# Two weight units interleaved k-tile by k-tile at the start of both feed-forward stages

## The reference

```python
h = rmsnorm(x, norm_ffn_g[layer]) * (1 + scale2) + shift2
x = x + gate2 * conv_ffn(h, w_ffn_gate[layer], w_ffn_up[layer], ffn_conv[layer], w_ffn_down[layer])

def conv_ffn(h, w_gate, w_up, conv, w_down):
    u = dwconv3(h @ w_gate, conv)
    return (jax.nn.silu(u) * (h @ w_up)) @ w_down
```

## Time and profile before

| | |
|---|---|
| median of 3 runs | 1585.81 us (1580.39 to 1587.88) |
| the profiled execution's own time | 1583.95 us |
| its span, first to last instruction | 1581.9 us |
| mean granted TensorE clock | 0.959 of full |
| TensorE busy | 1430.3 us (90%) |
| VectorE busy | 995.3 us (63%) |
| GpSimd busy | 658.7 us (42%) |

### The profile page before, as it was taken

The page is one execution under the profiler, slowest core; times in us unless marked ns, Lnnn a source line. Parts: engine busy times, 40 slices in busy tenths (PEclk is TensorE's granted clock), DMA queues, the critical chain, the costliest instruction groups (busy, mean ns, idle before and its releaser), DMA issues.

```text
span 1581.9 us, 24703 instructions
## 1 busy us (share of the span) xinstructions
PE 1430.3 (90%) x9517; PEld 1384.4 (88%) x9517; DVE 995.3 (63%) x1377; ACT 418.9 (26%) x725; POOL 658.7 (42%) x400
## 2 busy tenths in 40 slices
PE   3798789989868789999999999986999999999995
PEld 2598768989858689999999999975999999999995
DVE  5695477983568777687777888635655145415554
ACT  4615322146341253300110011156332011101122
POOL 0262344430204335555545555410454544455542
PEclk9799889999979889999999999998999999999998
DMA  9221411240213313543334433210332122222222
GB/s 377 94 94 53 147 40 41 90 151 28 79 73 142 120 54 126 189 146 138 123 116 149 146 138 121 83 45 1 102 110 93 67 80 79 65 82 70 75 70 78
DMA packets 44358, 161.13 MB, mean 102 GB/s; under 512 B 4752, under 2 KB 5904, under 8 KB 43280
## 3 DMA queue, kind: packets, MB, share of 16 engines
q1 hardware_dynamic: 44304, 160.43, 28.8%
HBM read 153.07 MB, written 5.77 MB: 100 GB/s over the span
## 4 chain that ended last, share of the span: by engine, by line
PE 75%; DVE 13%; issue 4%; ACT 4%; DMA 2%; POOL 1%; ACTq 0%; SPq 0%; DVEq 0%; POOLq 0%
PE ps L653 64%; PE ps L938 1%; DVE ada_raw L1430 1%; PE ps L665 1%; DVE outer L1620 1%; ACT work L1007 1%; DVE junk L1430 1%; DVE work L1447 1%; DVE blocks L1623 1%; PE ps L880 1%; PE ps L685 1%; DVE work L1350 1%; ACT work L1136 1%; PE ps L890 1%; DVE x L1385 1%
## 5 line engine op out<-in xcount | busy, mean ns | idle before, releaser
L582 POOL TENSOR_SCALAR whi<-raw 128x1024 fp32r<-128x1024 f32 (+1 forms) x172 | 192.3, 1118 | 763.9 <-PE ps L653 565.8
L653 PE MATMUL ps<-hhi,whi 128*128 128x320 f32 x1984 | 460.4, 314 | 52.4 <-DVE hlo L1414 31.0
L653 PE MATMUL ps<-hlo,whi 128*128 128x320 f32 x1984 | 455.7, 311 | 0.0
L653 PE MATMUL ps<-hhi,wlo 128*128 128x320 f32 x1984 | 455.2, 311 | 0.0
L585 POOL TENSOR_TENSOR wlo<-raw,whi 128x1024 fp32r<-128x1024 f32 (+1 forms) x172 | 435.6, 2532 | 14.4
L653 PEld LDWEIGHTS ps<-hhi,whi 128*128 128x128 f32 x1984 | 334.5, 190 | 61.4 <-issue 26.4
L653 PEld LDWEIGHTS ps<-hlo,whi 128*128 128x128 f32 x1984 | 335.5, 190 | 0.0
L653 PEld LDWEIGHTS ps<-hhi,wlo 128*128 128x128 f32 x1984 | 335.4, 190 | 0.0
L653 PE MATMUL ps<-hidhi,whi 128*128 128x320 f32 x704 | 161.2, 310 | 4.5 <-POOL wlo L585 3.1
L653 PE MATMUL ps<-hidlo,whi 128*128 128x320 f32 x704 | 161.0, 310 | 0.0
L653 PE MATMUL ps<-hidhi,wlo 128*128 128x320 f32 x704 | 160.9, 310 | 0.0
(11 more groups left out here) (205 smaller groups left out, 1318.7 us busy)
## 6 DMA issues: line engine op xcount, KB each, us to landing
raw<-in_w_gu SPq DMA_DIRECT2D x88, 512.0 KB, 3.2
ada_raw<-in_w_rows SPq DMA_DIRECT2D x75, 512.0 KB, 3.4
raw<-in_w_in SPq DMA_DIRECT2D x28, 512.0 KB, 3.3
raw<-in_w_dn SPq DMA_DIRECT2D x32, 448.0 KB, 3.3
ada_first<-in_w_ada SPq DMA_DIRECT2D x4, 2048.0 KB, 21.1
raw<-in_w_dn SPq DMA_DIRECT2D x16, 512.0 KB, 3.3
raw<-in_w_out SPq DMA_DIRECT2D x8, 512.0 KB, 4.6
x<-in_x SPq DMA_DIRECT2D x1, 2560.0 KB, 9.0
```

Source lines behind the costliest of these rows:

```text
L582: nc.gpsimd.tensor_scalar(whi[s][:, 0:n], raw[s][:, 0:n], 1.0, 0.0, ALU.mult, ALU.add).then_inc(s_whi, 1)
L653: last = nc.tensor.matmul(pair[pr][:, b], wt[s][:, cs], act[:, k, b * HALF:(b + 1) * HALF], start=(j == 0 and q == 0), stop=(j == len(tile ...
```

## The change

Three things, the same in both layers.

1. `first_units` takes units 0 and 1 together. For each k-tile TensorE waits for the normed tile k, makes unit 0's product of k (pair A), then unit 1's product of k-1 (pair B). After the last tile it makes unit 1's last product. Then come units 2 and 3, one after the other, outside the loop; the loop goes on from pair 2.
2. Unit 2 is split into a third pair of buffers (`whi2`, `wlo2`), laid over the last part of `rows_tok`, which the second layer's mixer uses.
3. The split of unit 2 has no guard on unit 0 any more; in its place POOL waits for the last normed tile (`s_h`). The split of unit 3 keeps its buffer and its guard: units 0 and 1 must both have been multiplied.

```diff
+        whi.append(nc.alloc_sbuf_tensor_at("whi2", [P, SLOT], F32R, offset=o4 - 8 * SLOT))
+        wlo.append(nc.alloc_sbuf_tensor_at("wlo2", [P, SLOT], F32R, offset=o4 - 4 * SLOT))
...
-            def split(u, half_u, s, n=SLOT, guard=True):
+            def split(u, half_u, s, n=SLOT, guard=True, to=None):
+                to = s if to is None else to
                 pool.wait_ge(s_raw[s], half_u * 16 + 16)
                 if guard:
                     pool.wait_ge(s_unit, u - 1)
...
+            def second_pair(u):
+                split(u + 2, u // 2 + 1, 0, guard=False, to=2)
+                split(u + 3, u // 2 + 1, 1)
...
                 for g, nf in enumerate(GROUPS):
-                    split_pairs(SEG["up", layer, g]["u"], nf)
+                    u = SEG["up", layer, g]["u"]
+                    if g == 0:
+                        for s in range(2):
+                            split(u + s, u // 2, s)
+                        pool.wait_ge(s_h, PRIMED + 16 + 8 * layer)
+                        second_pair(u)
+                    split_pairs(u, nf, first=(2 if g == 0 else 0))
                     split_pairs(SEG["down", layer, g]["u"], 4, nf * P)
...
+            def product(pr, s, tile, act_hi, act_lo, k, first, final):
+
+                cs = slice(tile * P, tile * P + P)
+                for q, (wt, act) in enumerate(((whi, act_hi), (whi, act_lo), (wlo, act_hi))):
+                    for b in range(2):
+                        last = nc.tensor.matmul(pair[pr][:, b], wt[s][:, cs], act[:, k, b * HALF:(b + 1) * HALF],
+                                                start=(first and q == 0), stop=(final and q == 2))
+                return last
...
+            def first_units(u, a, b, wait_k):
+
+                pe.wait_ge(s_split, u + 1)
+                pe.wait_ge(s_ev["A"], a)
+                for k in range(KD + 1):
+                    if k < KD:
+                        wait_k(k)
+                        last = product("A", 0, k, hhi, hlo, k, k == 0, k == KD - 1)
+                        if k == KD - 1:
+                            last.then_inc(s_unit, 1)
+                    if k == 1:
+                        pe.wait_ge(s_split, u + 2)
+                        pe.wait_ge(s_ev["B"], b)
+                    if k:
+                        last = product("B", 1, k - 1, hhi, hlo, k - 1, k == 1, k == KD)
+                last.then_inc(s_unit, 1)
+                for s in range(2):
+                    pe.wait_ge(s_split, u + 3 + s)
+                    pe.wait_ge(s_ev["AB"[s]], (a, b)[s] + 1)
+                    products("AB"[s], (2, 1)[s], range(KD), hhi, hlo, range(KD)).then_inc(s_unit, 1)
...
                     hr = 8 if layer == 0 else 16
-                    with pe.Fori(0, nf) as i:
+                    if g == 0:
+                        first_units(b["u"], b["A"], b["B"], lambda k: pe.wait_ge(s_h, PRIMED + hr + k + 1))
+                    with pe.Fori(2 if g == 0 else 0, nf) as i:
                         for s in range(2):
                             pe.wait_ge(s_split, i * 2 + (b["u"] + s + 1))
                             pe.wait_ge(s_ev["AB"[s]], i + b["AB"[s]])
-                            wait_k = (lambda j: pe.wait_ge(s_h, PRIMED + hr + j + 1)) if s == 0 and g == 0 else None
-                            products("AB"[s], s, range(KD), hhi, hlo, range(KD), wait_k).then_inc(s_unit, 1)
+                            products("AB"[s], s, range(KD), hhi, hlo, range(KD)).then_inc(s_unit, 1)
```

More of the change, by code:

```diff
@@ L430, in ada_split @@
         def ada_split(n):
-            return (whi + more[0:2])[n % 4], (wlo + more[2:4])[n % 4]
+            return (whi[0:2] + more[0:2])[n % 4], (wlo[0:2] + more[2:4])[n % 4]
         block = ctx.enter_context(nc.Block())
@@ L581, in split @@
                 pool.sem_inc(s_go, 1)
-                nc.gpsimd.tensor_scalar(whi[s][:, 0:n], raw[s][:, 0:n], 1.0, 0.0,
+                nc.gpsimd.tensor_scalar(whi[to][:, 0:n], raw[s][:, 0:n], 1.0, 0.0,
                                         ALU.mult, ALU.add).then_inc(s_whi, 1)
                 pool.wait_ge(s_whi, u + 1)
-                nc.gpsimd.tensor_tensor(wlo[s][:, 0:n], raw[s][:, 0:n], whi[s][:, 0:n].bitcast(F32),
+                nc.gpsimd.tensor_tensor(wlo[to][:, 0:n], raw[s][:, 0:n], whi[to][:, 0:n].bitcast(F32),
                                         ALU.subtract).then_inc(s_split, 1)
@@ L649, in products @@
                         wait_k(j)
[L650 to L656, removed]
-                return last
+                    last = product(pr, s, tile, hi, lo, k, j == 0, j == len(tiles) - 1)
+                return last
+            def first_units(u, a, b, wait_k):
[17 more added lines that the diff above has]
+                    products("AB"[s], (2, 1)[s], range(KD), hhi, hlo, range(KD)).then_inc(s_unit, 1)
             def ada(n):
```

## The result

The changed kernel takes 1586.59 us, the median of 22 runs (1579.65 to 1591.27), against 1582.31 for 22 runs of the kernel before: ratio 1.003, 95% interval 1.0016 to 1.0044. It is slower by some 0.3%, about 4.7 us. I had forecast 1585.3 us and a step of -0.5 us. The time lies in the range given and the step is inside the 0.5% that I took as no change, but it has the wrong sign and the runs resolve it. That 1585.3 comes so near to 1586.59 is luck: it stands on the median of the first three runs of the kernel before, 1585.81, which lies 3.5 us above that of all 22. Two repeats of the same kernel beside later experiments gave 1.0011 (0.9997 to 1.0025) and 1.0023 (1.0002 to 1.0044), and the kernel before measured against itself gave 1.001 (0.9999 to 1.0022).

The account below looks back on a forecast made before the run. TensorE was taken as the bound, short of clock and input at the layer's start. Layer 0's +1.1 and layer 1's -1.6 us sum to -0.5, from the median 1585.81 to 1585.3 us; range 1579.8 to 1589.5.

Parts of the forecast that it names:

- The first two units: Start of each layer's stage: TensorE's 16 products without gaps, ending 3.1 us earlier in layer 0, 3.5 in layer 1.
- unit 2's wait: Unit 2 waits for pair A; of layer 0's 3.1 us 2.57 are left, and layer 1's unit 2 starts 3.0 earlier.
- Unit 3's wait for pair B: POOL and VectorE take turns, so pair B frees late; unit 3 starts 1.2 us earlier in layer 0, 1.6 in layer 1.
- The cover holds: Rival: pair B's reader is in time and both layers keep unit 2's gain, -5.6 us, 1580.2; chance 0.12.
- Unit 5 of layer 0: Unit 5 waits about 2.3 us for pair B and starts 1.1 us later than before, so layer 0 loses.
- Only unit 3 waits: Rival: VectorE catches up before pair 1, so unit 5 has no wait; -2.8 us, 1583.0; chance 0.19.
- Layer 1: Layer 1's first units: unit 3 starts 1.6 us earlier and unit 5 keeps that gain, -1.6 us.
- The clock falls in a new wait: Rival: TensorE's clock halves after new waits, one fall giving +1.1 us, three +4.3; 1586.9 to 1590.1; chance 0.13.
- The added straight-line code I take at nothing: TensorE's written-out units cost 0 us, issuing the same matmuls and waits; lateness would show as idle time put down to issue.
- from there all is as before, shifted: Layer 0 behind pair 2: 2.41 us of VectorE idle time absorbs its lateness, and later work only shifts.
- +1.1 - 1.6 = -0.5 us: Sum over both stages: layer 0 1.1 us later, layer 1 1.6 earlier, together -0.5 us.

Follow-up runs that it names:

- the last one with all edits: Changed kernel, unit 3's split after pair 0's convolution, layer 0's units 4 and 5 written out, rows moved in groups 0 and 1: ratio 0.9979 to kernel before.
- split behind the convolution: Changed kernel, with POOL's split of unit 3 made to wait for pair 0's convolution: ratio 0.999 to the kernel before.
- layer 0 only: Kernel before with the change made in layer 0 alone, for POOL and TensorE alike: ratio 1.0009.
- after, group 1's rows: Changed kernel with one row sum of layer 0's group 1 moved from its last pair to an earlier one: ratio 0.9987 to the kernel before.
- the pair with group 1's rows moved: Kernel before and changed kernel, each with one row sum of layer 0's group 1 moved to an earlier pair: ratios 0.9966 and 0.9987 to the kernel before.
- the control: The kernel before run again unchanged, against itself: ratio 1.001.
- after, one pair more: Changed kernel with units 4 and 5 of layer 0 also written out ahead of TensorE's loop: ratio 1.001 to the kernel before.
- the moved row: Kernel before with one row sum of layer 0's group 1 moved from its last pair to an earlier one: ratio 0.9966.

## Why the prediction was wrong, by its own steps

**The first two units: right, but for the clock.** No gap, and unit 2's wait of 0.48 us (0.55 forecast). The full clock came 3.3 us into the stage, not 5.6: in 556.81 to 560.1 the matmuls are slow, and those of 559.62 the last ones lengthened. I had called a denser start that brings the clock back sooner possible, and had left it out of the sum. The denser start is not what did it: by the granted clock the return comes 3.2 to 4.0 us into layer 0's stage in 14 of the 16 profiles, all repeats with the old start among them, and at 5.9 and 6.1 us in two, the first profile of the kernel before and the last one with all edits. I had taken an odd moment for the rule. The kernel before does not feel it (48.31 us to unit 7's split with 5.9 us and with 3.3), since its first unit goes at the pace of the normed tiles; the changed one does, 0.45 us for each. So unit 3 gained 2.2 us where I had 1.2: at my 5.6 us it would start at 24.61 + 0.45 x 2.36 = 25.67 us, and the forecast was 25.63.

**Unit 3's wait for pair B: the mechanism right.** 1.05 us against 1.4 forecast, in layer 1 1.08. POOL and VectorE took turns as worked out: in the changed kernel's timeline of both engines `whi` goes ahead of the convolution's first instruction (0.55 us when alone), and the first pair of SCALAR_TENSOR_TENSOR goes with `wlo`, 3.03 us instead of 1.01:

```profile
572.79 1.05 POOL L585 TENSOR_SCALAR whi<-raw 128x1024 fp32r<-128x1024 f32 x1 [0.67 <-issue]
572.97 1.21 DVE L1482 TENSOR_SCALAR work<-work,cols 128x640 f32<-128x640 f32 x1 [4.59 <-ACT work L1371]
573.91 2.52 POOL L588 TENSOR_TENSOR wlo<-raw,whi 128x1024 fp32r<-128x1024 f32 x1
574.21 3.03 DVE L1485 SCALAR_TENSOR_TENSOR work<-work,cols 128x511 f32<-128x511 f32 x2
...
580.45 0.82 DVE L1855 TENSOR_TENSOR work<-work,ps 128x640 f32<-128x640 f32 x1 [2.16 <-ACT work L1374]
```

The split behind the convolution proves it: without POOL in the chain the lengths are bare and unit 3's wait is gone in both layers. "The cover holds" is refuted. The rule that I had quoted from the Trainium skill (SBUF — State Buffer, "Who interferes with whom"), an exclusive lock held for the whole instruction, agrees with the 3.03 us.

**Unit 5 of layer 0: right in kind, 0.9 us too dear.** The wait is 2.18 us (2.3 forecast), the balance +0.2 instead of +1.1, and the clock's earlier return, worth 1.06 us, is the whole difference. "Only unit 3 waits" is refuted.

**Layer 1: -1.1 instead of -1.6 us.** Unit 3 gained 1.2 instead of 1.6, and its stretch 1.1. Here the clock came later than I had read, 5.9 us into the stage instead of 5.1, which makes 0.35 of the 0.4; in the third profile of the changed kernel it came after 5.3 us, and unit 3 started at +25.53 us instead of +25.83.

**The clock falls in a new wait: the threshold was wrong.** I had written that it decides once a wait comes to 3 us, from one fall after 3.06 us, and none after 2.21 and 3.15. Among the eight profiles with layer 0's part and a wait ahead of unit 5 it fell in three, after 2.22 us and 1.88 us ("layer 0 only", "split behind the convolution") and in "after, group 1's rows"; in the five others it did not, the changed kernel's own 2.18 us among them, though in "after, group 1's rows" it fell behind a wait of the same 2.18 us. A fall costs 1.4 to 1.6 us (unit 5's start to unit 7's split takes 8.9 to 9.1 us with it and 7.5 without). The place of the 3.15 us is no different: all 16 profiles have a wait of 2.95 to 3.91 us there, and behind it the clock fell in twelve, behind 2.98 us in one and not behind 3.27 us in another; behind the wait of 2.21 us it fell in three of the 16. So this rival is no case of its own but a part of the forecast, worth about 0.6 us on the mean. The Trainium skill (TensorE: Matmul & The Clock Gate, "Part 1") says that where the clock changes varies from run to run; these profiles agree.

**The step that failed: "The added straight-line code I take at nothing", and with it "from there all is as before, shifted".** The code costs nothing where it stands: no wait of the matmuls from 556 to 622 us is put down to issue, which is what I had said would show it. (The page's chain has issue at 5% instead of 4%; that is the chain, which now runs through ScalarE and VectorE there, with 1.2 us of each ACT_TABLE_LOAD called issue.) Its price comes 273 us later: 192 more matmuls in TensorE's program of layer 0 move the packets of TensorE's instructions, one of them falls on a row load and a weight load that had no cover before either, and the wait grows from 3.06 us (3.00 to 3.40 in six profiles without the packet there) to 4.87 (4.05 to 4.87 in six with it). Together with the clock behind it that is +0.8 to +2.8 us. I had the row for the wait in hand and used it only to price the clock; that TensorE stood there for a load meant that anything which delays the load by a microsecond delays the end by one.

**The balance.** For the two stages I had +1.1 - 1.6 = -0.5 us, and +0.3 - 1.1 = -0.8 came out: two misses by the moment of the clock that happen to point opposite ways. Over the whole kernel it is: layer 0's units +0.3, or up to +2.2 with a fall; the down units +0.8 to +2.8; layer 1 -1.1: 0 to +3.9 us, about +2 for the usual case. The three ratios say +1.7 to +4.7 us. What is left, 1 to 2 us, stays open: it is of the size by which the control differs from one, and the time to the first product of layer 0, code that no edit here touches, lay anywhere from 548 to 564 us in the 16 profiles, so that single profiles can't tell whether the longer program also costs something there. That the packet delays the loads rests on where it stands in the profiles, six with and six without it, on the kernels that moved it by code length alone, and on the pair with group 1's rows moved. How 16 KB come to cost 1 to 1.8 us was not measured, and the packet is not the only thing that makes such a load late: in "after, one pair more", without a packet near, the next row and weight loads took 4.7 and 5.4 us to land.

## What to carry to other kernels

Before you call written-out code free, look for waits on a DMA anywhere behind it, also far behind: those are the places that a shifted instruction fetch lengthens, and a few us of uncovered load there can be worth more than the change itself, as the moved row showed. When a buffer is freed through VectorE, see what POOL does at the same time, and let POOL wait until the instructions that matter are through, if its own result isn't needed for a while. Cut both profiles at equal marks and look at every stretch, not at the place of the edit alone. And take a second profile of the kernel before: one more would have shown that the clock's return, read from a single one, was the odd case.

## What the hardware showed that I had not expected

- A TensorE wait of 1.88 us can be enough for the granted clock to fall to the half level, while one of 3.27 us left it up in another profile. Waits of 2.18 us ahead of the same unit did both. The slow stretch behind a fall was 2.8 to 5.5 us long in the down units, with no relation to the length of the wait.
- Packets of 16 KB on the instruction queue coincide with 1 to 1.8 us longer landings of loads of 448 KB and 512 KB: in the first two profiles 3.4 against 5.2 us for the row, and from 4.5 to 6.3 us between issue and use for the weights.
- The moment at which the full clock comes back at the start of layer 0's stage was 3.2 to 4.0 us into it in 14 profiles and 5.9 and 6.1 us in two, with the dense start and with the gaps of the kernel before alike. It shifts a stretch by up to 1.2 us (44.93 against 46.14 us), as much as the effects that were looked for here.
